# A new VectorE order in the SSD windows, and GpSimd's state update in operations of 512 columns

## The reference, cut to what matters

```
xbc  = silu(causal conv, 4 taps, of h @ w_in)          # x: 2 tiles, B and C: 1 tile each
dt   = softplus(h @ w_dt + bias);   a = dt * A          # per head
# prompt, chunks of 128 tokens:
y    = ((C B^T) * decay) (dt x)  +  exp(a_cum) * (C h_prev)        # "diagonal" + "off-diagonal"
h    = exp(a_last) * h_prev + (decay_to_end * dt x)^T B            # chunk states, 4 steps
# each of the 8 samples, one token:
h    = exp(dt A) * h0  +  (dt x) outer B                            # state, stored as an output
y    = sum over the state of  h * C
# both:
y    = (y + D x) * silu(z);   y = y * rsqrt(mean of squares over the group) * g
out  = out + y @ w_out
```

## Time and profile before

| what | us |
|---|---|
| median of 3 runs (lowest, highest) | 1680.85 (1678.82, 1683.0) |
| the profiled execution, its time | 1682.01 |
| its span | 1680.3 |
| TensorE busy | 1571.3 (94%), mean granted clock 0.972 |
| VectorE, ScalarE, GpSimd busy | 909.1, 618.4, 374.0 |
| the eight windows and the half output product | about 76 to 601 us of the span |

### The profile page before, as it was taken

The page is one execution under the profiler, slowest core; times in us unless marked ns, Lnnn a source line. Parts: engine busy times, 40 slices in busy tenths (PEclk is TensorE's granted clock), DMA queues, the critical chain, the costliest instruction groups (busy, mean ns, idle before and its releaser), DMA issues.

```text
span 1680.3 us, 30210 instructions
## 1 busy us (share of the span) xinstructions
PE 1571.3 (94%) x12653; PEld 1545.7 (92%) x12653; DVE 909.1 (54%) x1020; ACT 618.4 (37%) x827; POOL 374.0 (22%) x431
## 2 busy tenths in 40 slices
PE   6898878979987899999999999999999999999996
PEld 5898877879886799999999999999999999999996
DVE  3477688772876785343444453464455535344353
ACT  5656646622665242121212343342233212122221
POOL 1067576650665730000000022200001000000001
PEclk9999898989998999999999999999999999999998
DMA  5354445343544332332232332222223232233221
GB/s 151 93 158 127 138 129 164 118 133 94 147 125 136 107 104 81 96 101 91 85 100 76 101 114 89 76 77 89 89 76 101 76 101 89 89 99 98 78 76 51
DMA packets 158910, 173.19 MB, mean 103 GB/s; under 512 B 13912, under 2 KB 146896, under 8 KB 158784
## 3 DMA queue, kind: packets, MB, share of 16 engines
q1 hardware_dynamic: 137032, 131.30, 25.6%
q0 software_dynamic: 9472, 26.50, 5.6%
q10 hardware_dynamic: 12288, 13.71, 2.8%
HBM read 159.53 MB, written 12.21 MB: 102 GB/s over the span
## 4 chain that ended last, share of the span: by engine, by line
PE 63%; DVE 1%; ACT 1%; issue 0%; POOL 0%; ACTq 0%; DVEq 0%
PE ps L510 61%; PE ps L859 1%; PE ps L530 1%; PE ps L827 0%; PE ps L774 0%; PE ps L553 0%; DVE w_lo L1551 0%; PE ps L625 0%; POOL ssum L1415 0%; ACT arena L1359 0%; ACT w_hi L914 0%; PE ps L899 0%; PE ps L851 0%; POOL arena L1483 0%; DVE work L1557 0%
## 5 line engine op out<-in xcount | busy, mean ns | idle before, releaser
L510 PE MATMUL ps<-h_hi,w_hi 128*128 128x260 f32 (+2 forms) x2320 | 482.0, 289 | 5.2 <-issue 4.6
L510 PE MATMUL ps<-h_lo,w_hi 128*128 128x260 f32 (+2 forms) x2320 | 472.0, 285 | 0.0
L510 PE MATMUL ps<-h_hi,w_lo 128*128 128x260 f32 (+2 forms) x2320 | 471.9, 285 | 0.0
L1551 DVE TENSOR_TENSOR w_lo<-w,w_hi 128x2048 fp32r<-128x2048 f32 (+2 forms) x122 | 280.3, 2298 | 183.2 <-ACT w_hi L914 183.2
L510 PEld LDWEIGHTS ps<-h_hi,w_hi 128*128 128x128 f32 x2320 | 365.4, 192 | 7.8 <-issue 5.8
L510 PEld LDWEIGHTS ps<-h_lo,w_hi 128*128 128x128 f32 x2320 | 363.5, 191 | 0.0
L510 PEld LDWEIGHTS ps<-h_hi,w_lo 128*128 128x128 f32 x2320 | 363.2, 191 | 0.0
L914 ACT ACTIVATE w_hi<-w 128x2048 fp32r<-128x2048 f32 (+2 forms) x122 | 229.3, 1879 | 326.9 <-PE ps L510 326.7
L510 PE MATMUL ps<-a_hi,w_hi 128*128 128x260 f32 x1504 | 307.2, 286 | 9.2 <-DVE a_lo L1642 5.3
L510 PE MATMUL ps<-a_hi,w_lo 128*128 128x260 f32 x1504 | 305.5, 285 | 0.0
L510 PE MATMUL ps<-a_lo,w_hi 128*128 128x260 f32 x1504 | 305.0, 285 | 0.0
(11 more groups left out here) (208 smaller groups left out, 1370.4 us busy)
## 6 DMA issues: line engine op xcount, KB each, us to landing
w<-in_mlp_w_up SPq DMA_DIRECT2D x32, 1024.0 KB, 5.7
w<-in_mlp_w_down SPq DMA_DIRECT2D x32, 1024.0 KB, 5.2
w<-in_ssd_w_in SPq DMA_DIRECT2D x16, 1024.0 KB, 6.4
w<-in_cm_w_in SPq DMA_DIRECT2D x16, 1024.0 KB, 5.7
w<-in_ssd_w_in SPq DMA_DIRECT2D x16, 512.0 KB, 6.6
arena<-in_state_ssm POOLq DMA_DIRECT2D x64, 128.0 KB, 3.8
arena<-scr_a ACTq DMA_DIRECT2D x16, 512.0 KB, 3.9
arena<-scr_bc POOLq DMA_DIRECT2D x32, 256.0 KB, 3.9
```

The source lines that it names most:

```text
L510: mm = pe.matmul(ps[:, 2 * slot + b, 0:tn], w[:, pair.slot, k, col:col + P], x[:, k, t0:t0 + tn], start=(k == 0 and n == 0), stop=(k == ti ...
L1551: nc.vector.tensor_tensor(w_lo[:, pair.slot, k, w], w32[:, pair.slot, k, w], w_hi[:, pair.slot, k, w].bitcast(F32), ALU.subtract).then_inc ...
```

## The change

VectorE's window is put in another order. The scaling (L1765, now L1763), with the second `y_diag`, stands before the second `conv` and the split; `sample` 0 stands behind that split; `conv` 2 behind `states`, `sample` 1 behind it. `combine` is cut in two: the off-diagonal part (`combine`, L1703 and L1708) stands before `conv` 3, and the samples' part with the two closing products (`gate`, L1715 and L1722) comes last, behind `sample` 2 and 3. TensorE's two waits for `comb_done` at L636 and before it become waits for `cchain`, the off-diagonal multiplications; ScalarE's `abc_load` waits for `yadd_done`. GpSimd makes the outer products of both tiles in one operation of 512 columns into `rstd` (free in layer 0's mixer) and their sums in another; the counts of `state_added` are halved everywhere.

Core of the diff (new semaphores and halved counts left out):

```diff
-        outer = carve(2, N)
+        outer = rstd[:, 0:4 * N]
...
@@ PE state_out(g)
-                pe.wait_ge(comb_done, 2 * g + 1)
+                pe.wait_ge(cchain, 2 * g + 1)
...
@@ PE window(g)
-                    pe.wait_ge(comb_done, 2 * g - 1)
+                    pe.wait_ge(cchain, 2 * g - 1)
...
@@ ACT abc_load(g, i)
-                        act_e.wait_ge(comb_done, 2 * g)
+                        act_e.wait_ge(yadd_done, 2 * g)
...
@@ POOL window(g)
-                    for i in range(2):
-                        k = 2 * n + i
-                        if due(k):
-                            pool.wait_ge(state_added, k)
-                        nc.gpsimd.tensor_tensor(outer[:, :, :], bcs[:, n % 2, :, 0:N],
-                                                xdts[:, i, b0:b0 + 2].unsqueeze(2).broadcast_to([P, 2, N]), ALU.mult)\
-                          .then_inc(outer_done, 1)
-                        pool.wait_ge(outer_done, k + 1)
-                        nc.gpsimd.tensor_tensor(state[:, 2 * i:2 * i + 2, :], state[:, 2 * i:2 * i + 2, :], outer[:, :, :],
-                                                ALU.add).then_inc(state_added, 1)
-                    pool.wait_ge(state_added, 2 * n + 2)
+                    if due(n):
+                        pool.wait_ge(state_added, n)
+                    nc.gpsimd.tensor_tensor(outer.rearrange("p (i b n) -> p i b n", i=2, b=2),
+                                            bcs[:, n % 2, :, 0:N].unsqueeze(1).broadcast_to([P, 2, 2, N]),
+                                            xdts[:, :, b0:b0 + 2].unsqueeze(3).broadcast_to([P, 2, 2, N]), ALU.mult)\
+                      .then_inc(outer_done, 1)
+                    pool.wait_ge(outer_done, n + 1)
+                    nc.gpsimd.tensor_tensor(state.rearrange("p j n -> p (j n)"), state.rearrange("p j n -> p (j n)"), outer,
+                                            ALU.add).then_inc(state_added, 1)
+                    pool.wait_ge(state_added, n + 1)
...
@@ DVE combine(g), gate(g)
                 for i in range(2):
-                    n = 3 * (2 * g + i)
                     dve.wait_ge(yoff_done, 2 * g + i + 1)
                     dve.wait_ge(ef_done, 2 * g + i + 1)
                     nc.vector.tensor_tensor(abc[:, 0, i, CH:TP], ps[:, 5 + i, CH:TP], abc[:, 0, i, CH:TP], ALU.mult)\
                       .then_inc(cchain, 1)
-                    if i == 0:
-                        dve.wait_ge(sred_done, 4 * g + 4)
+                for i in range(2):
+                    dve.wait_ge(cchain, 2 * g + i + 1)
+                    dve.wait_ge(y1_done, 2 * g + i + 1)
+                    nc.vector.tensor_tensor(work[:, i, CH:TP], work[:, i, CH:TP], abc[:, 0, i, CH:TP], ALU.add)\
+                      .then_inc(yadd_done, 1)
+
+            def gate(g):
+
+                dve.wait_ge(sred_done, 4 * g + 4)
+                for i in range(2):
...
+                for i in range(2):
+                    dve.wait_ge(ysmp_done, 2 * g + i + 1)
+                    dve.wait_ge(yadd_done, 2 * g + i + 1)
                     dve.wait_ge(evac_done, Pair(group_pair(g, 2)).unit(i, 1))
                     nc.vector.tensor_tensor(work[:, i, :], work[:, i, :], zs[:, i, :], ALU.mult)\
                       .then_inc(comb_done, 1)
```

More of the change, by code:

```diff
@@ L337, in hybrid_step @@
         comb_done = sem("comb_done")
+        yadd_done = sem("yadd_done")
+        ysmp_done = sem("ysmp_done")
         ysq_done = sem("ysq_done")
@@ L1731, in window @@
                 if due(4 * g):
-                    dve.wait_ge(state_added, 8 * g)
+                    dve.wait_ge(state_added, 4 * g)
                 dve.wait_ge(silu_done, 4 * g + 4)
@@ L1750, in window @@
                     y_low(g - 1)
-                    sample(g, 0)
-                if not more:
                     evac_out(0)
@@ L1757, in window @@
                     conv(nxt, 0)
-                if not more:
-                    evac_out(1)
-                sample(g, 0 if more else 1)
-                split_w(Pair(group_pair(nxt, 1) + 1 if more else J_OUT1 + 2))
-                if more:
-                    conv(nxt, 1)
                 dve.wait_ge(ydiag_done, 2 * g + 2)
@@ L1769, in window @@
                 y_diag(g, 1)
+                if more:
+                    conv(nxt, 1)
+                else:
+                    evac_out(1)
+                split_w(Pair(group_pair(nxt, 1) + 1 if more else J_OUT1 + 2))
+                sample(g, 0)
                 if not more:
                     evac_out(2)
-                if more:
-                    sample(g, 1)
-                if more:
-                    conv(nxt, 2)
                 if g == 0:
@@ L1778, in window @@
                 states(g)
-                sample(g, 2)
+                if more:
+                    conv(nxt, 2)
+                sample(g, 1)
                 if not more:
                     evac_out(3)
+                combine(g)
                 if more:
                     conv(nxt, 3)
+                sample(g, 2)
                 sample(g, 3)
-                combine(g)
+                gate(g)
             dve.wait_ge(par_landed, 48)
```

11 lines of the change are left out of this document (3 added, 8 removed).

## The result

The changed kernel took 1709.49 us (median of 4 runs, 1706.8 to 1712.72) against 1679.84 us of the kernel before (4 runs, 1678.57 to 1683.0): the ratio is 1.0174, 95% interval 1.0149 to 1.02. So it is slower by 1.7%, and the time lies above the range of the prediction. The side was right; the size (+7.05 us) was a quarter of what came (+24.8 us between the profiled executions, 1682.01 and 1706.8).

The account below looks back on a forecast made before the run. The prediction took a ring of waits through VectorE and GpSimd, 59 us a window, as the bound, not TensorE's waits. Its window terms summed to +7.05 us on 1682.01, so 1689.1; the median 1.16 lower gave 1687.9, range 1674 to 1699.

Parts of the forecast that it names:

- The ring: Layer 0's mixer windows: closing product, squares, samples' B and C out and back, four steps, `sample` 3, closing product; 59 us.
- the hold: GpSimd's load for step 2 waits some 5 us at its queue's head until VectorE has multiplied sample 0.
- The fourth rival: TensorE's waits simply go, or windows turn without waiting for `sample` 0: 41 us less in six windows, 1647; chance 0.08.
- Reciprocal after zero: VectorE's reciprocal, counted from the end of the previous group's first closing product: 13.61 less 1.10, so 12.51 us.
- The 1.2 us taken off behind window 7: After window 7's closing product the squares come in a row: 1.2 us less, turning +6.6 into +5.4.
- the landing of step 2's load: Middle window: load lands 7.4 us after the split, at 41.39 after the previous first closing product; bounds 39.67 and 42.80.
- The third rival: Longer GpSimd operations hold VectorE longer: 1.8 us in six windows, +10.8, 1698.7; chance 0.10.
- the 0.25 that the forecast had added for slow `decayed`: Middle windows: period 58.35 taken as 58.6, since group 3's `decayed` took 5.30 against group 2's 3.53.
- From window 4 to 5: Output product 1.2 us closer to the first closing product (-1.2), then window 5, starting with TensorE: +0.6.
- Window 0: First window: scaling waits for the diagonal products until 106.46, closing product at 137.2 against 133.55: +3.65 us.
- Window 7: Last window: `sample` 0 now behind the diagonal products, 58.9 against 52.27: +6.6, less 1.2, so +5.4 us.
- rival 1: Step 2's loads are not held by the weights, landing 3.00 us after issue: -12.2 in seven windows, 1675.7; chance 0.15.

Follow-up runs that it names:

- e1: Changed kernel with sample 0's product back at its old place (behind `conv` 0; in window 7 between `y_low` and `evac_out(0)`): 1655.66 us, ratio 0.9864 to the kernel before.
- e2: Changed kernel with ScalarE's 512 KB `abc_load` issued ahead of the two silu steps instead of behind `ef_exp`: 1695.9 us, ratio 1.0095 to the kernel before.
- e9: Changed kernel with sample 0's product ahead of the second split and `abc_load` ahead of the silu steps: 1668.57 us, ratio 0.9938 to the kernel before.
- e3: Kernel before with only GpSimd's outer product and sum in operations of 512 columns, VectorE's old order: 1658.23 us, ratio 0.9875 to the kernel before.
- e4: Changed kernel with GpSimd's operations in pairs of 256 columns again, so VectorE's new order alone: 1717.65 us, ratio 1.0232 to the kernel before.
- e8: Kernel before with VectorE's second split behind `conv` 1, so the weights are asked for 2.4 us later: 1668.13 us, ratio 0.993 to the kernel before.
- e7: Changed kernel with sample 0's product back at its old place in window 7 alone: 1699.27 us, ratio 1.0129 to the kernel before.
- e5: Changed kernel with sample 0's product ahead of the second split, still behind `conv` 1: 1678.72 us, ratio 1.0 to the kernel before.

## Why the prediction was right and where it was wrong

**The ring and the hold: right.** GpSimd waits at L1450 for L1660 in all eight windows, 6.06 in group 2's. TensorE's two waits left their lines and came back larger at L673. e1 shows it from the other side: with the hold gone from step 2, 54 us go. The fourth rival's 1647 us (no hold) was within 9 us of what e1 gave. But the sign of the total was partly luck. In windows 1 to 4 I forecast a period 0.35 us shorter than before, and it became 2.2 longer; the forecast came out slower only by windows 0 and 7.

**The terms that came out.** Reciprocal after zero: 12.36, forecast 12.51. The outer product 1.04 and the sum 1.26 us undisturbed (1.35 and 1.65 beside VectorE), forecast 1.03 and 1.27. `conv` 0's end to the end of sample 0's multiplication: 6.93 (229.59 to 236.52), forecast 7.03. Step 2's start to the closing product's end: 61.16 - 44.31 = 16.85 in the mean of windows 1 to 4, forecast 16.96. The 1.2 us taken off behind window 7, as the squares come in a row, came too (5.38 to 4.18).

**The step that failed: the landing of step 2's load ("I take 7.4, so 41.39").** Step 2 starts at 43.90, 44.52, 45.09 and 43.73 after zero in windows 1 to 4, in the mean 44.31; the text had 41.39, and 42.80 as its upper bound. Of the 2.92 us (the upper bound would have left 1.51),

- 1.44 is the landing itself. From the start of the states' load to step 2 it took 7.58 in the mean, and the text made it 6.14. The text counted the old landing from the split (7.14) and not from the load's own issue (7.55 in the same rows), and so let a load that goes out later behind its split land faster. But the old load had the weights 0.56 behind it and `abc_load` well behind; the new one has both ahead, and its first packet starts 3.3 to 3.8 us after the issue. e2 gives 0.87 of the landing to `abc_load`; e2 against e9 gives 2.5 to the place of the weights.
- 1.2 is VectorE: sample 0's multiplication ends at 35.87 in the mean instead of 34.68. In windows 1, 2 and 4 `conv` 0 beside the longer GpSimd operations takes 0.98 more (4.12 for 3.14; e3 and e1 have it, e4 and e8 don't). In window 3 it takes 2.77, but starts 3.0 us later than in the others, behind a `decayed` of 6.15. The third rival had this mechanism at 1.8 us a window; it is about half that and comes on top of the forecast, not in place of it.
- 0.3 is the gap between that multiplication (236.52) and the issue on GpSimd (236.83), counted as nothing.

Less 0.11 behind step 2 and the 0.25 that the forecast had added for slow `decayed`, that makes 2.56 us a window at the closing product: the period was 61.16 for 58.6, or 10.25 us over windows 1 to 4. From window 4 to 5 it was +1.68 for a forecast of -0.6 (2.3 us), in window 6 +1.35 for 0.

**Window 0** came out at +6.95 for +3.65. The text took 7.4 behind the split for the new landing, and that again was short (8.04 from the load's issue). The old landing was 4.43 us there, shorter than the 7.55 of group 2's window, since the weights went out 2.37 us behind the load. Both prices of a landing stood in the trace of before, in windows 0 and 3 against window 2, and what set them apart was how soon the weights came behind the load. Window 3 of the kernel before, first GpSimd, then SyncE:

```profile
284.39 1.43 POOL L1441 DMA_DIRECT2D arena<-in_state_ssm  x2
289.11 1.23 POOL L1469 TENSOR_TENSOR arena<-arena,dtf 128x512 f32<-128x512 f32 x1 [3.29 <-DMA arena<-in_state_ssm]
```

```profile
287.17 0.37 SPq L413 DMA_DIRECT2D w<-in_ssd_w_in  x1
```

**Window 7** came out at +8.12 for +6.6 at the closing product (the +5.4 of the text has the 1.2 behind it taken off): the multiplication ended at 38.1 instead of 36.9, and the landing took 5.24 from the start of the issue, where 4.42 was counted, the price of a load with no weights beside it. Here too the weights were 1.39 ahead.

The differences (3.3, 10.25, 2.3, 1.35 and 1.5) make 18.7 us. The profiled executions differ by 24.8 where the sum had 7.05, so by 17.75 more; what follows window 7 gave one back.

**The range** failed with the same step. Its lower end was a landing free of the weights (rival 1), its upper end the hold on VectorE (rival 3) on top of a landing of 41.39. The later landing, 42.80, which the text itself gave as a bound, was in neither end, and nothing later than it was thought of: a load behind the weights and a third transfer. Both errors came, one on the other. The first rival (loads not held by the weights) is wrong for this order and describes what other orders get: 4.1 to 5.0 us with the weights 2.4 us or more behind. The Trainium skill ("DMA: Bandwidth & Descriptors", "Queues, rings and completion order") has each DMA engine take turns between its queues, packet by packet; by that a load would get its share at once, as the first rival took it. The trace does not show that: with the weights ahead, the first packet of the loads started 2.84 us after the issue in e2 and 3.54 in the kernel after, and 0.71 in e9, where they were behind (group 2's window each). Why the loads' packets come so late, no run shows. Nor was the gain of GpSimd's 512 columns sized well by the step's own time: 3.1 of e3's 4.6 us are a landing that escapes a collision.

## What to carry to other kernels

When an edit moves the issue of a load on the critical ring, list what every other queue issues within some microseconds of its new time, count the landing from the load's own issue, and price it by a load with the same neighbours, ahead as well as behind. An operation that frees a buffer for another engine's next load belongs directly behind its operands, ahead of anything that triggers a large transfer. A wait of the bottleneck engine is not a gain to be had until you know the ring that it waits in; here 52 us of TensorE's waits left their lines, and 64 us stood at another one.

## What the runs showed of the hardware

- A state load for step 2 (256 KB, with 256 KB of `bcs` just ahead of it on the same queue) landed 4.1 to 5.0 us after its issue began when the 1 MB of weights came 2.4 us or more behind it. It took 7.3 to 7.6 with the weights 0.6 to 0.8 behind (kernel before), 5.9 to 7.1 with them 1.4 ahead (e2), and 6.9 to 8.9 with the 512 KB of `abc_load` near as well (kernel after, e4, e7). With the 512 KB issued together with it and the weights 2.1 behind it took 5.4 to 7.5 (e5). Asking for the weights later made the kernel faster (e8).
- The packets came nearly in the order of the issues: with the weights 1.4 us ahead, SyncE's queue had moved 846 (kernel after) and 910 (e2) of 1024 KB before the first packet of GpSimd's loads, in group 2's window.
- A GpSimd outer product took 0.61 us for 256 and 1.04 for 512 columns, a sum 0.72 and 1.26, undisturbed: one operation saves 0.18 on both products of a step and 0.18 on both sums, and beside VectorE's convolutions both engines slow down, neither for the whole of the other's operation (1.35 for 1.04, and 4.12 for three convolutions that take 2.42 alone).
